# Expert weights in runs of eight rows, and gathered tokens one to a partition, in a fused diffusion-transformer step

## What is computed

```
g_prob, g_idx = lax.top_k(jax.nn.softmax(gl, axis=-1), 1)          # 1 of 4 groups
e_prob, e_idx = lax.top_k(jax.nn.softmax(el_sel, axis=-1), MOE_TOP_K)  # 2 of 8 experts
...
a = jnp.einsum('td,edf->tef', x, P['w_e_gate'][l, g])              # 1024 -> 256
b = jnp.einsum('td,edf->tef', x, P['w_e_up'][l, g])                # 1024 -> 256
hid = jax.nn.silu(a) * b * combine[:, g, :, None]
y = y + jnp.einsum('tef,efd->td', hid, P['w_e_down'][l, g])        # 256 -> 1024
```

## Time and profile before

| | us |
|---|---|
| median of three runs | 1169.92 |
| profiled execution, its own time | 1170.78 |
| its span, first to last instruction | 1169.1 |
| first gather issued | 862.10 |
| first transpose of gathered tokens | 868.56 |
| last `down` ends | 1126.75 |
| TensorE busy | 1041.0 (89% of the span) |
| mean granted TensorE clock | 0.949 |

### The profile page before, as it was taken

One profiled execution on the slowest core, in us unless ns is written; L12 is line 12 of the kernel. 1 busy time (PEld: TensorE's weight loads), 2 busy tenths in 40 slices (PEclk: granted clock), 3 DMA queues, 4 the chain that ended last, 5 costly groups with the idle time before them and its releaser, 6 DMA issues.

```text
span 1169.1 us, 13722 instructions
## 1 busy us (share of the span) xinstructions
PE 1041.0 (89%) x5215; PEld 627.3 (54%) x5215; DVE 452.0 (39%) x1081; ACT 215.8 (18%) x388; POOL 232.1 (20%) x285
## 2 busy tenths in 40 slices
PE   4999999999999999999998999999549999869750
PEld 2467757776566666656655555445435545434320
DVE  4656674144754744744742000022423111101118
ACT  4110001000333333333300000011101111101014
POOL 3040000100770001110111411022112543213114
PEclk9999999999999999999999999999659999979885
DMA  9931220333341332242233910111789999999954
GB/s 313 362 86 45 72 72 1 120 96 108 87 123 61 121 113 74 73 144 73 77 125 129 308 36 36 36 72 73 269 339 390 364 376 407 406 406 406 403 208 166
DMA packets 101153, 209.75 MB, mean 179 GB/s; under 512 B 8984, under 2 KB 64614, under 8 KB 100960
## 3 DMA queue, kind: packets, MB, share of 16 engines
q1 hardware_dynamic: 87984, 179.18, 42.6%
q0 software_dynamic: 13072, 29.67, 7.1%
q10 hardware_dynamic: 32, 0.01, 0.0%
HBM read 197.77 MB, written 18.72 MB: 185 GB/s over the span
## 4 chain that ended last, share of the span: by engine, by line
PE 80%; DMA 6%; SPq 5%; DVE 4%; issue 3%; ACT 1%; POOL 0%; POOLq 0%; DVEq 0%
PE pair L1689 24%; PE pair L1696 13%; PE pair L1688 7%; PE pair L1913 6%; PE pair L1989 5%; PE pair L1692 4%; DMA dft_region<-in_w_e_up 4%; PE pair L1835 3%; SPq L652 3%; PE pair L2006 3%; PE pair L1899 2%; PE pair L1812 2%; PE pair L2018 2%; SPq L642 2%; PE pair L1775 1%
## 5 line engine op out<-in xcount | busy, mean ns | idle before, releaser
L1689 PE MATMUL pair<-hT_region,ring_region 128*128 128x512 f32 x544 | 282.7, 602 | 0.0
L1688 PEld LDWEIGHTS pair<-hT_region,ring_region 128*128 128x128 f32 x544 | 102.8, 192 | 124.2 <-issue 122.8
L1688 PE MATMUL pair<-hT_region,ring_region 128*128 128x128 f32 x544 | 107.3, 279 | 1.8 <-DVE hT_region L1388 1.5
L829 POOL TENSOR_TENSOR dft_region<-dft_region,padded_region 128x640 f32<-128x640 f32 x24 | 36.9, 1538 | 346.2 <-DVE padded_region L1315 346.2
L1689 PEld LDWEIGHTS pair<-hT_region,ring_region 128*128 128x128 f32 x544 | 83.8, 195 | 0.0
L1989 PE MATMUL pair<-ring_region,padded_region 128*64 128x256 f32 x640 | 73.5, 382 | 4.4 <-DMA ring_region<-in_w_e_up 4.4
L1315 DVE TENSOR_TENSOR padded_region<-pair,padded_region 128x640 f32<-128x640 f32 x24 | 19.8, 824 | 142.8 <-PE pair L1899 99.6
L1913 PE MATMUL pair<-ring_region,dft_region 128*128 128x512 f32 x160 | 71.3, 605 | 2.6 <-issue 2.6
L1629 DVE TENSOR_TENSOR mixer_region<-pair,mixer_region 128x128 f32<-128x128 f32 x34 | 9.9, 291 | 153.8 <-ACT mixer_region L1065 153.8
L1036 ACT ACTIVATE padded_region<-pair,colv 128x640 f32<-128x640 f32 x32 | 25.4, 794 | 234.5 <-PE pair L1689 234.5
L854 POOL DMA_INDIRECT moe_pairs<-padded_region,bias_region x34 | 34.2, 1005 | 171.7 <-DVE padded_region L1641 165.7
(11 more groups left out here) (372 smaller groups left out, 1621.3 us busy)
## 6 DMA issues: line engine op xcount, KB each, us to landing
ring_region<-in_w_ada SPq DMA_DIRECT2D x24, 1024.0 KB, 7.1
ring_region<-in_w_gate SPq DMA_DIRECT2D x16, 1024.0 KB, 5.6
ring_region<-in_w_in SPq DMA_DIRECT2D x13, 1024.0 KB, 5.5
ring_region<-in_w_e_gate SPq DMA_DIRECT2D x12, 1024.0 KB, 12.7
ring_region<-in_w_e_up SPq DMA_DIRECT2D x12, 1024.0 KB, 19.2
ring_region<-in_w_e_down SPq DMA_DIRECT2D x24, 512.0 KB, 14.5
hT_region<-in_w_e_gate SPq DMA_DIRECT2D x7, 1024.0 KB, 11.9
hT_region<-in_w_e_up SPq DMA_DIRECT2D x7, 1024.0 KB, 19.2
```

Source lines behind the costliest of these rows:

```text
L829: pool.tensor_tensor(merged[:, dj, :], merged[:, dj, :], gtmp, ALU.add).then_inc(merged_add, 1)
L1688: mm(ps_[0:m, W0:W0 + TC], lhsT, rhs[:, 0:TC], start=start, stop=stop)
L1689: return mm(ps_[0:m, W0 + TC:1024], lhsT, rhs[:, TC:T], start=start, stop=stop)
```

## The change

The input channel is laid out as `(p k)`: partition p holds the eight consecutive rows 8p to 8p + 7 of gate and of up, one run of 8 KB for each matrix. To match, a gathered token row stays whole: a block's 64 tokens go to 64 partitions with 1024 floats each, even buffers to partitions 0 to 63, odd ones to 64 to 127. The turning is eight plain products (not transposes) with a 64 x 64 piece of the identity as moving operand and every eighth float of the rows as stationary operand. DVE makes three further index tables with whole token numbers for the gathers; the scatters keep their half rows.

```
-        xg = [RY[:, HD2 * i:HD2 * (i + 1)] for i in range(BUFS)]
+        xg = [RY[CAP * (i % 2):CAP * (i % 2 + 1), D * (i // 2):D * (i // 2 + 1)] for i in range(BUFS)]
-            wg = I["w_e_gate"].rearrange("l g e (h p k) f -> (l g e) p h (k f)", h=2, p=P)
-            wu = I["w_e_up"].rearrange("l g e (h p k) f -> (l g e) p h (k f)", h=2, p=P)
+            wg = I["w_e_gate"].rearrange("l g e (p k) f -> (l g e) p (k f)", p=P)
+            wu = I["w_e_up"].rearrange("l g e (p k) f -> (l g e) p (k f)", p=P)
...
             def gather(b, idx_ap):
-                pool.indirect_dma_start(xg[b], None, hid_rows, bass.IndirectOffsetOnAxis(ap=idx_ap, axis=0),
-                                        bounds_check=2 * NPAIR - 1, oob_is_err=False).then_inc(xg_full[b], 16)
+                pool.indirect_dma_start(xg[b], None, hid_d, bass.IndirectOffsetOnAxis(ap=idx_ap[0:CAP], axis=0),
+                                        bounds_check=NPAIR - 1, oob_is_err=False).then_inc(xg_full[b], 16)
...
                     computed(dve, st)
+                    put(ts(whole_pair.bitcast(U32), ps(st)[:, 2 * EXPERTS:2 * EXPERTS + PAIRED // 2], 2.0 * NPAIR, None, ALU.add))
+                    for b in range(2):
+                        put(ts(whole[b].bitcast(U32), ps(st)[:, EXPERTS * b:EXPERTS * (b + 1)], 2.0 * NPAIR, None, ALU.add))
...
                 if not isinstance(drained_x, int) or drained_x > 0:
                     pe.wait_ge(xT_free, drained_x)
-                for kt in range(4):
-                    ins = turn(MX[u][:, P * kt:P * (kt + 1)], xg[b].rearrange("r (p k) -> r k p", k=4)[:, kt, :])
+                half = slice(CAP * (b % 2), CAP * (b % 2 + 1))
+                for kt in range(KD):
+                    ins = mm(MX[u][:, CAP * kt:CAP * (kt + 1)], xg[b].rearrange("r (p k) -> r k p", k=KD)[:, kt, :],
+                             ident[half, half], start=True, stop=True)
                 ins.then_inc(xT_full, 1)
...
-                        ins = mm(MG[u][CAP * f:CAP * (f + 1), 0:2 * P], xgT[u][:, kt % 4, kt // 4, :],
+                        ins = mm(MG[u][CAP * f:CAP * (f + 1), 0:2 * P], xgT[u][:, kt, :],
```

More of the change, by code:

```diff
@@ L429, in build @@
         idx = [RB[:, EXPERTS * b:EXPERTS * (b + 1)] for b in range(2)]
-        idxo = RB[:, 64:66]
+        idxo = RB[:, 64:67]
+        whole = [RB[:, 1568 + EXPERTS * b:1568 + EXPERTS * (b + 1)] for b in range(2)]
+        whole_pair = RB[:, 624:624 + PAIRED // 2]
         slotu = RB[:, 70:80]
@@ L559, in build @@
                  (RR[:, 6144:10240], RR[:, 10240:11264], RR[:, 11264:12288])]
-        wsets = [(ab.rearrange("p (g h x) -> p g h x", g=2, h=2),
+        wsets = [(ab.rearrange("p (g x) -> p g x", g=2),
                   ab.rearrange("p (g k f) -> p k g f", g=2, k=KD), c) for ab, *c in wsets]
@@ L564, in build @@
         USES = [len(range(u, NBLK, BUFS)) for u in range(BUFS)]
-        xg = [RY[:, HD2 * i:HD2 * (i + 1)] for i in range(BUFS)]
+        xg = [RY[CAP * (i % 2):CAP * (i % 2 + 1), D * (i // 2):D * (i // 2 + 1)] for i in range(BUFS)]
         sil, hid, hidT = ([RY[:, 2 * D + P * (2 * n + i):2 * D + P * (2 * n + i + 1)] for i in range(2)]
                           for n in range(3))
-        xgT = [RP[:, 2 * D + HD2 * i:2 * D + HD2 * (i + 1)].rearrange("p (k h b) -> p k h b", k=4, h=2)
+        xgT = [RP[:, 2 * D + HD2 * i:2 * D + HD2 * (i + 1)].rearrange("p (k b) -> p k b", k=KD)
                for i in range(2)]
@@ L585, in build @@
         FC_PS, FL_PS = pair_ps[2][:, 2 * P:3 * P], pair_ps[2][:, HD2 + 2 * P:HD2 + 3 * P]
+        whole_ready = sem("further_tokens_ready")
         ov_idx_in, ov_idx_ready = sem("further_idx_in"), sem("further_idx_ready")
@@ L642, in load_one @@
                 sp.dma_start(dst, src[e] if isinstance(e, int) else
-                             src[bass.ds(e, 1)].rearrange("a p k n -> (a p) k n")).then_inc(done, 16)
+                             src[bass.ds(e, 1)].rearrange("a p n -> (a p) n")).then_inc(done, 16)
             def load_up(e, s, done):
@@ L845, in _ @@
                 computed(pool, ("hT", t))
-            hid_rows = hid_d.rearrange("n (h d) -> (n h) d", h=2)
             out_rows = out_d.rearrange("n (h d) -> (n h) d", h=2)
             def gather(b, idx_ap):
-                pool.indirect_dma_start(xg[b], None, hid_rows, bass.IndirectOffsetOnAxis(ap=idx_ap, axis=0),
-                                        bounds_check=2 * NPAIR - 1, oob_is_err=False).then_inc(xg_full[b], 16)
+                pool.indirect_dma_start(xg[b], None, hid_d, bass.IndirectOffsetOnAxis(ap=idx_ap[0:CAP], axis=0),
+                                        bounds_check=NPAIR - 1, oob_is_err=False).then_inc(xg_full[b], 16)
             def scatter(b, idx_ap):
@@ L855, in scatter, with tokens_of @@
                                         bounds_check=2 * NPAIR - 1, oob_is_err=False).then_inc(y_sent[b], 16)
+            def tokens_of(n):
+                at, b = BLOCK[n]
+                if len(at) == 2:
+                    j = (at[0] - FIRST) // EVERY
+                    return whole_pair.bitcast(U32)[:, j:j + 1]
+                return whole[b].bitcast(U32)[:, at[0]:at[0] + 1]
             def rows_of(n):
@@ L867, in _ @@
             for n in range(BUFS):
-                gather(n, rows_of(n))
+                gather(n, tokens_of(n))
             for n in range(NBLK):
@@ L872, in _ @@
                     pool.wait_ge(xT_full, n + 1)
-                    gather(n % BUFS, rows_of(n + BUFS))
+                    gather(n % BUFS, tokens_of(n + BUFS))
                 pool.wait_ge(dn_free, n + 1)
@@ L900, in _ @@
                     pool.wait_ge(ov_idx_ready, i + 1)
+                    pool.wait_ge(whole_ready, i + 1)
                     step_over()
-                    gather(0, idxo[:, 1:2].bitcast(U32))
+                    gather(0, idxo[:, 2:3].bitcast(U32))
                     pool.wait_ge(dn_free, i + (NBLK + 1))
@@ L1058, in turned @@
                     act.wait_ge(gu_full, n - 1)
-                act.activation(xgT[u].rearrange("p k h b -> p (k h b)"), MX[u], ACT.Copy).then_inc(xT_free, 1)
+                act.activation(xgT[u].rearrange("p k b -> p (k b)"), MX[u], ACT.Copy).then_inc(xT_free, 1)
             def silu(n, u):
@@ L1658, in _ @@
                     dve.wait_ge(ov_idx_in, i * 32 + 32)
+                    dve.tensor_copy(idxo[:, 2:3].bitcast(U32), idxo[:, 0:1]).then_inc(whole_ready, 1)
                     ts(idxo[:, 1:2].bitcast(U32), idxo[:, 0:1], 2.0, c_("half_"), ALU.mult, ALU.add
@@ L2018, in up_two @@
                             ins = mm(MG[u][at:at + HALFCAP, 0:2 * P],
-                                     xgT[u][:, kt % 4, kt // 4, HALFCAP * i:HALFCAP * (i + 1)],
+                                     xgT[u][:, kt, HALFCAP * i:HALFCAP * (i + 1)],
                                      wsets[s][1][:, kt, :, P * f:P * (f + 1)], start=(kt == 0), stop=(kt == KD - 1),
```

## The result

The change makes the kernel slower, by some eleven times the forecast amount: 1316.93 us is the median of four runs (1309.58 to 1319.26), against 1170.68 us for the kernel before (four runs beside them, 1169.28 to 1172.73). The ratio is 1.1234, with a 95% interval of 1.1197 to 1.1271. Forecast were 1183.5 us and a range of 1175 to 1206. The direction is right, the size is far out.

What follows compares the result with a forecast made beforehand. Weights bound the expert stage's end; the longer turn makes TensorE the bound. Profiled 1170.78 + 13.5 = 1184.3 us, less 0.9 for the median: 1183.5 us, range 1175 to 1206.

Steps and rivals of the forecast that it cites:

- The bound: Expert stage: weights bind at the end, TensorE has some 40 us of reserve; after the change TensorE binds.
- Part 4: Turning of tokens on TensorE: 16 loads at 0.122 us, turn 0.68 to 2.10 us, growth 1.42 (1.18 to 2.27).
- Rival A: Turning loads: stride costs its full 68 ns or step eight costs more; turn 2.95, 1210.7 us; chance 0.20 with in-between cases.
- The sum: TensorE chain in the expert stage: 32 blocks of 7.83 us without gaps, last `up` at 1131.9, 13.5 us longer.
- Part 2: Token gathers to 64 partitions: same bytes in half as many runs, landing covered by early issue; cost 0.
- Rival B: Turning loads: stride wholly hidden, turn 1.86, 1175.7 us, or 1180.3 if gathers cost 13 us of DMA; chance 0.12.
- Part 1: Gate and up weight loads: longer runs save 2.5 us (0 to 5), counting only where weights end the wait.
- Part 3: DVE's three more index instructions ahead of the first gather: +0.55 us, once.
- Part 5: ACT's copy, SiLU and DVE's product stay hidden under TensorE work; nothing new is late but TensorE itself.
- The start: Stage start to second `up`: DVE +0.55, first turn +2.4, second +1.4, first `up` -1.3; together +3.05 us, to 881.3.
- Rival C: Expert stage: weights stay the bound and longer runs pay, turn under 1.68; 1167.4 to 1164.9 us; chance 0.05.
- D: Weight loads: 8 KB runs are cut to 4 KB pieces, nothing saved; time as forecast, within its 0.58 chance.

Runs made afterwards that it cites:

- experiment 2: The kernel before, with its four transposes of gathered tokens written as plain products: 1183.31 us, ratio 1.0124.
- experiment 9: The changed kernel with each turn cut in two, its halves behind the halves of `up`: 1262.44 us, ratio 1.0789 against the kernel before.
- experiment 3: The changed kernel, its turning products reading 128 contiguous columns instead of every eighth float: 1195.61 us, ratio 1.0226 against the kernel before.
- experiment 10: The changed kernel, its turning products reading every second float instead of every eighth: 1195.48 us, ratio 1.0218 against the kernel before.
- experiment 5: The kernel before with only gate and up weights rearranged into 8 KB runs, old gathers and transposes kept: 1167.88 us, ratio 0.9959.
- experiment 1: The changed kernel with its eight turning products written as transposes, layout kept: 1187.16 us, ratio 1.016 against the kernel before.
- experiment 6: The changed kernel with eight transposes for the turning products and weights back in 4 KB runs: 1188.08 us, ratio 1.0134 against the kernel before.
- experiment 7: The kernel before with 8 KB weight runs, half-row gathers kept, rows written in permuted order so transposes read contiguous columns: 1169.56 us, ratio 0.998.

## Why the prediction was wrong

**The bound** was read rightly: weights gave way to TensorE, and the reserve of some 40 us was all there was to spend.

**Part 4 failed first,** in the sentence "I take 0.122 a load, near the strided transposes' pace, since a plain load that is already slow hides most of the stride". It measured 0.240. The price of the stride was read from a transpose and carried over to a plain product; experiment 2 shows the same data with the same step at 0.13 us as a transpose and 0.239 as a plain load. The upper end failed with it: 68 ns added to a load isn't a bound, where the plain load takes twice its time. Rival A named the cause, and its sign, loads of over 250 ns, stands in the trace (332), but it got 2.95 us instead of 4.00 for the same reason. Rows that priced a plain float32 load with a step did not stand in the trace, and the range should have reached to a doubling: 16 x 0.214 + 0.15 = 3.57 us a turn, 1183.5 + 1.47 x 33 = 1232 us. Even that is short of the time, by the clock.

**The sum failed second,** in its premise, given without a reason, that a TensorE without gaps keeps its clock ("a clock of 1.00 from 880 to 1130"). The chain puts 67 us on it, and experiment 9 gets 54.5 of the 146 back, the passages that it adds paid: the loss is there with 4 us of turning in one piece, and gone with two pieces of 2. Why the clock falls stays open. With the turn as forecast (2.1 us) the premise would have held, as experiments 2, 3 and 10 show; the second miss hangs on the first.

**Part 2 was wrong and hidden.** "Cost 0" is what the change shows in the stage, where DMA has room. Nor were there "half as many runs": the packets of q0 stayed at 13072. The first gather already took 9.32 instead of 6.33 us (7.33 to 9.91 in the runs with the same gathers, and 7.64 in experiment 5 with the old ones), and with a fast turn (experiments 1, 3, 6 and 10) weights become the bound again at 368 to 378 GB/s. Rival B's price of 13 us for it was near the 16 to 18 measured (experiments 6 and 1).

**Part 1 was right:** 413 GB/s and 0.27 to 0.54% of the time (experiment 5), where 2.5 us were forecast for a bound by weights and about 4 measured (2.3 in experiment 7). **Part 3 was right** within 0.3 us: the two added lines take 0.17 and 0.19, but the old ones now 0.13 and 0.33 instead of 0.22 and 0.33. **Part 5** held: no copy is late.

**The start:** +9.6 us to the second `up` (887.89 against 878.28) and not +3.05. The gather's landing is 3.0 of it, the first turn 2.9 instead of 2.4, the second 3.3 instead of 1.4, and the first `up`, which should have gained 1.3, took 6.50, at a clock of 0.56 over its length where it had 0.58 before: with 2.9 us more of turning ahead of it the clock came back no sooner. That first turn also says something of the load. It ran at a granted clock of 0.50 and took 4.05 us, hardly more than the later ones at 1.00 (4.00), while with contiguous columns (experiment 3) it took 3.66 us at 0.50 and 1.93 at 1.00. So the price of the step isn't a number of TensorE's cycles, and doubling the load at half the clock, as the sum did, was right for contiguous columns only.

**Rival C** fell with the turn, and **D** is false. Before, 193 of 101153 packets had 8 KB or more; now 8388 have (92964 - 84576), and there are 8189 packets fewer (64 matrices x 128 partitions are 8192):

```profile
DMA packets 92964, 209.79 MB, mean 159 GB/s; under 512 B 8996, under 2 KB 64626, under 8 KB 84576
```

From step to step the medians (the kernel before had medians of 1169.2 to 1171.9 us beside them, so each step is good to some 2 us) read: plain products instead of transposes in the old layout +14 (experiment 2, of 45 us of work that the reserve mostly took in); the same pace with the new gathers +12 more (10); the step past 16 bytes +67 (9), the clock +54.5, with the split's own cost already taken off (the change).

## What to carry to other kernels

Price a strided operand from rows of the same kind of instruction, and if there are none let the range reach to a doubling: a transpose's loads say nothing of a plain float32 product's. When TensorE becomes the bound, don't carry its full clock into the new rhythm; ask what stands in one piece, and split long runs of loads with few moving columns between streaming ones, without taking apart products that run beside each other. And price a cost that is hidden today for the day when its cover is gone: the gathers' took 12 to 18 us as soon as DMA was the bound again.

## What the runs showed of the hardware

- A plain float32 load of 128 columns takes 0.111 us with contiguous columns, 0.117 with 8 bytes from column to column, 0.233 with 16 and 0.240 with 32. A transpose's load took 0.109 with 32 bytes. Why the transpose escapes is open. With 32 bytes a turn took 4.05 us at a clock of 0.50 and 4.00 at 1.00, with contiguous columns 3.66 and 1.93.
- The clock fell to half right behind 4 us of such loads though TensorE was never idle, and it stayed at 1.00 with the same loads in pieces of 2 us between halves of `up`. In pieces of 1.1 us between single `down` products it was at 0.93 in the mean and fell at times. With twice the moving columns in seven of eight products of the same 4 us it was at 0.86 instead of 0.79. What exactly is measured there is open.
- Full DMA queues moved 406 GB/s in 4 KB runs and 413 with 8 KB ones; with the gathers landing in 64 partitions 378 and 373, at the same share of 1.02 to 1.03. The share alone does not show such a loss.
- One product with an output of 64 x 512 alone costs 1.00 us at the full clock, where four in a row, into the two halves of the partitions by turns, cost 1.87.
